# Products of 512 and of 256 columns issued in groups of six blocks that run on across the weight units, in place of groups of eight

## What is computed

```
x  = x + fox_mixer(rms_norm(x), w_in, ...) @ w_out          # 2048 -> 3*2048, 2048 -> 2048
x  = x + (silu(conv(rms_norm(x) @ w_up_gate)) * conv(... @ w_up_val)) @ w_down   # 2048 -> 2*5632, 5632 -> 2048
x  = x + concat(gla_mixer(h, ...), dilated_mixer(h, ...)) @ w_out                # the second block, same widths
x  = x + (silu(h2 @ w_gate) * (h2 @ w_up)) @ w_down
```

## Time and profile before

| | |
|---|---|
| median of 3 runs | 2276.18 us (2275.83 to 2277.05) |
| the profiled execution | 2276.7 us; its span (first to last instruction) 2274.8 us |
| TensorE matmul busy | 2260.0 us, 99% of the span, 13190 instructions |
| VectorE busy | 1623.9 us, 71% |
| ScalarE busy | 1230.4 us, 54% |
| granted TensorE clock | 0.999 of full speed over the span |
| DMA | 421.82 MB, mean 185 GB/s |

### The profile page before, as it was taken

How to read it: one execution, slowest core, us unless ns; L and a number is a source line. 1 busy time by engine, 2 the same in 40 slices (tenths; PEclk the granted TensorE clock), 3 DMA queues, 4 the chain that set the end, 5 groups by cost and what they waited for, 6 DMA issues and landing times.

```text
span 2274.8 us, 39123 instructions
## 1 busy us (share of the span) xinstructions
PE 2260.0 (99%) x13190; PEld 1980.8 (87%) x13190; DVE 1623.9 (71%) x2378; ACT 1230.4 (54%) x1614; POOL 53.1 (2%) x78
## 2 busy tenths in 40 slices
PE   8999999999999999999999999999999999999999
PEld 6888888888888888888888888888888888888888
DVE  7877777888888888555567577777666676664554
ACT  6777765655555555444465577655444444443332
POOL 1111100000000000000000000000000000000000
PEclk9999999999999999999999999999999999999999
DMA  6555555555555555655545555555555555555654
GB/s 203 193 176 183 183 169 191 187 193 191 189 192 185 193 189 186 198 194 187 192 154 187 161 168 166 168 192 190 190 193 188 190 192 188 191 191 199 203 198 134
DMA packets 118593, 421.82 MB, mean 185 GB/s; under 512 B 13773, under 2 KB 15973, under 8 KB 118544
## 3 DMA queue, kind: packets, MB, share of 16 engines
q1 hardware_dynamic: 113760, 413.19, 55.2%
q0 software_dynamic: 2048, 5.39, 0.9%
q10 hardware_dynamic: 2736, 2.58, 0.3%
HBM read 418.98 MB, written 3.70 MB: 186 GB/s over the span
## 4 chain that ended last, share of the span: by engine, by line
PE 98%; DVE 1%; ACT 0%; DMA 0%; issue 0%; SPq 0%; DVEq 0%
PE acc L378 63%; PE acc L381 32%; PE b_score L435 0%; PE b_turn L440 0%; DMA xres<-xt 0%; PE b_mean L425 0%; PE b_mean L446 0%; PE b_mean L426 0%; PE b_val L432 0%; PE b_mean L447 0%; PE b_score L434 0%; PE b_mean L448 0%; ACT xs L857 0%; PE b_mean L518 0%; PE b_mean L515 0%; PE b_score L502 0%
## 5 line engine op out<-in xcount | busy, mean ns | idle before, releaser
L729 ACT ACTIVATE whi<-raw 128x1024 fp32r<-128x1024 f32 x783 | 826.3, 1059 | 826.0 <-PE acc L381 815.1
L1053 DVE TENSOR_TENSOR wlo<-raw,whi 128x1024 fp32r<-128x1024 f32 x783 | 959.9, 1229 | 376.3 <-ACT whi L729 374.3
L378 PE MATMUL acc<-xs,whi 128*128 128x512 f32 x4344 | 1094.9, 395 | 2.2 <-DVE wlo L1053 1.8
L378 PEld LDWEIGHTS acc<-xs,whi 128*128 128x128 f32 x4344 | 781.9, 188 | 146.5 <-issue 5.1
L381 PEld LDWEIGHTS acc<-xs,wlo 128*128 128x128 f32 x4344 | 583.4, 188 | 44.3
L381 PE MATMUL acc<-xs,wlo 128*128 128x256 f32 x4344 | 593.9, 279 | 0.0
L378 PE MATMUL acc<-hid,whi 128*128 128x512 f32 x1408 | 351.0, 392 | 0.0
L1059 DVE TENSOR_REDUCE folded_t<-acc 128x256 f32<-128x512 f32 x336 | 231.9, 690 | 137.9 <-PE acc L381 128.2
L378 PEld LDWEIGHTS acc<-hid,whi 128*128 128x128 f32 x1408 | 251.9, 188 | 43.2
L381 PEld LDWEIGHTS acc<-hid,wlo 128*128 128x128 f32 x1408 | 188.3, 188 | 14.4
L381 PE MATMUL acc<-hid,wlo 128*128 128x256 f32 x1408 | 191.6, 278 | 0.0
(11 more groups left out here) (190 smaller groups left out, 1001.6 us busy)
## 6 DMA issues: line engine op xcount, KB each, us to landing
raw<-wstream SPq DMA_DIRECT2D x783, 512.0 KB, 4.0
decay_row<-decay_scratch POOLq DMA_DIRECT2D x16, 128.0 KB, 3.7
out<-xres ACTq DMA_DIRECT2D x16, 128.0 KB, 2.4
xres<-xt SPq DMA_DIRECT2D x3, 512.0 KB, 8.4
dist_scratch<-bias_scratch POOLq DMA_DIRECT2D x8, 192.0 KB, 4.6
toeplitz<-dist_scratch POOLq DMA_DIRECT2D x8, 128.0 KB, 3.9
xres<-xt SPq DMA_DIRECT2D x2, 256.0 KB, 4.6
raw<-wstream SPq DMA_DIRECT2D x2, 256.0 KB, 5.6
```

The source lines that it names most:

```text
L378: pe.matmul(acc[bank_no][:, :], w_hi, x[:, kc, :, :].rearrange("p a s -> p (a s)"), start=first, stop=False)
L729: act.activation(whi[slot][:, :], raw[slot][:, :], ACT.Copy).then_inc(hi_ready, 1)
L1053: dve.tensor_tensor(wlo[slot][:, :], raw[slot][:, :], whi[slot][:, :], ALU.subtract).then_inc(lo_ready, 1)
```

## The change

TensorE's order alone is changed: which large products stand together before their small ones. The number of products, their operands, the banks and the work of every other engine are as before. `stretch` takes the list of all blocks between two pieces of other work, whatever units they lie in, and cuts it into groups of six blocks (`GROUP`): six large products, then the six small ones of the same blocks. The first group has four blocks where the call says so (behind `head_mean`, `head_turn` and some of the linear attention's pieces). What is left at the end of a list is one group if it is three blocks or fewer, and otherwise a group of three and one of the rest: for the lists of 64 blocks (the loop bodies of `project` and `up`) and of 352 blocks (`down`) that is a group of three and a group of one. `half` alone is cut 3, 3, 2. The waits (`lo_ready` at a unit's first block, `chunk_out` at a chunk's first) now stand before the block that needs them, so in the middle of a group too, and `unit_used` rises at the small product of the unit's last block.

```diff
+GROUP = 6
-            def unit(pos, k, blocks, x):
-                slot = pos.slot(k)
-                pe.wait_ge(lo_ready, pos.unit(k) + 1)
-                for j, (bank_no, kc, first, last, late) in enumerate(blocks):
...
-                    pe.matmul(acc[bank_no][:, :], w_hi, x[:, kc, :, :].rearrange("p a s -> p (a s)"), start=first, stop=False)
-                for j, (bank_no, kc, first, last, late) in enumerate(blocks):
...
-                mm.then_inc(unit_used, 1)
+            def unit_blocks(k, bank_no, part, free=None, late=None):
 
                 late = late or {}
+                return [(k, j, bank_no, 8 * part + j, part == 0 and j == 0, part == 1 and j == 7,
+                         free if part == 0 and j == 0 else None, late.get(8 * part + j)) for j in range(BLOCKS)]
+
+            def groups(n, first=GROUP):
+                sizes = [first] + [GROUP] * ((n - first) // GROUP)
+                rest = n - sum(sizes)
+                return sizes + ([3, rest - 3] if rest > 3 else [rest])
+
+            def stretch(pos, blocks, x, first=GROUP):
+
+                at = 0
+                for size in groups(len(blocks), first):
+                    for k, j, bank_no, kc, opens, closes, free, late in blocks[at:at + size]:
+                        if j == 0:
+                            pe.wait_ge(lo_ready, pos.unit(k) + 1)
+                        if free is not None:
+                            pe.wait_ge(chunk_out, free)
+                        if late:
+                            pe.wait_ge(*late)
+                        w_hi = whi[pos.slot(k)][:, j * P:(j + 1) * P]
+                        pe.matmul(acc[bank_no][:, :], w_hi, x[:, kc, :, :].rearrange("p a s -> p (a s)"), start=opens, stop=False)
+                    for k, j, bank_no, kc, opens, closes, free, late in blocks[at:at + size]:
+                        w_lo = wlo[pos.slot(k)][:, j * P:(j + 1) * P]
+                        mm = pe.matmul(acc[bank_no][:, S:2 * S], w_lo, x[:, kc, 0, :], start=False, stop=closes)
+                        if j == BLOCKS - 1:
+                            mm.then_inc(unit_used, 1)
+                    at += size
+
+            def half(pos, k, bank_no, part, x, late=None, first=3):
+                stretch(pos, unit_blocks(k, bank_no, part, None, late), x, first)
...
-                whole_q(0)
-                whole_q(1)
+                stretch(pos, unit_blocks(k0, 1, 0, chunk - 2) + unit_blocks(k0 + 1, 1, 1), xs, 4)
                 if lag >= 2:
                     head_values(n - 2, n)
                 if lag >= 1:
                     head_scores(n - 1)
-                whole(pos, k0 + 2, 2, chunk + 1)
-                pe.wait_ge(chunk_out, chunk)
-                half(pos, k0 + 4, 3, 0, xs)
+                stretch(pos, unit_blocks(k0 + 2, 2, 0, chunk - 1) + unit_blocks(k0 + 3, 2, 1) + unit_blocks(k0 + 4, 3, 0, chunk), xs)
                 if lag >= 1:
                     head_turn(n - 1)
-                half(pos, k0 + 5, 3, 1, xs)
+                half(pos, k0 + 5, 3, 1, xs, None, 4)
...
                 with pe.Fori(1, FC // 2) as i:
-                    pairs(Pos(layer.unit_up, 8, i), i, False)
+                    stretch(Pos(layer.unit_up, 8, i), units(i, 0, 8), xs)
```

More of the change, by code:

```diff
@@ L384, in half @@
-            def half(pos, k, bank_no, part, x, late=None):
-                late = late or {}
[L387 to L393, removed]
+            def unit_blocks(k, bank_no, part, free=None, late=None):
+                late = late or {}
+                return [(k, j, bank_no, 8 * part + j, part == 0 and j == 0, part == 1 and j == 7,
+                         free if part == 0 and j == 0 else None, late.get(8 * part + j)) for j in range(BLOCKS)]
@@ L453, in head @@
                 chunk = run.chunk0 + 3 * h
-                whole_q = lambda part: half(pos, k0 + part, 1, part, xs)
-                pe.wait_ge(chunk_out, chunk - 2)
-                whole_q(0)
-                whole_q(1)
+                stretch(pos, unit_blocks(k0, 1, 0, chunk - 2) + unit_blocks(k0 + 1, 1, 1), xs, 4)
                 if lag >= 2:
@@ L530, in gla_head, with units @@
                 chunk = L1.chunk_heads + 6 * g
[L531 to L537, removed]
+                def units(lo, hi, first=GROUP):
+                    blocks = []
+                    for k in range(lo, hi):
+                        c, part = divmod(k, 2)
+                        blocks += unit_blocks(k, 1 + c % 3, part, chunk + c - 2)
+                    stretch(pos, blocks, xs, first)
@@ L539, in project @@
+                units(0, 1)
+                gla_outputs(g - 1)
+                units(1, 3, 4)
+                gla_turn_out(g - 1)
+                units(3, 8)
+                gla_intra(g)
+                units(8, 10)
+                gla_turn_v(g, True)
+                units(10, 11)
+                gla_chunk_states(g)
+                units(11, 12, 4)
             def project(layer, run):
                 last = run.count0 + run.n - 1
-                between = {0: (lambda: head_values(last - 1, last + 1), lambda: head_scores(last)),
-                           2: (lambda: head_turn(last),), 3: (lambda: pe.wait_ge(head_copied, last), lambda: head_values(last, last + 1))}
@@ L545, in group @@
[L545 to L560, removed]
@@ L562, in project, with units @@
-                group(Pos(layer.unit_out), 0, True)
+                def units(i, lo, hi, late=None):
+                    blocks = []
+                    for k in range(lo, hi):
+                        part, c = divmod(k, 4)
+                        blocks += unit_blocks(k, c, part, layer.chunk_out + 4 * i + c - 3, late if k == lo else None)
+                    return blocks
+                pos = Pos(layer.unit_out)
+                if layer.n:
+                    pe.wait_ge(g_mixed, GLA_HEADS)
@@ new lines, in project @@
+                stretch(pos, units(0, 0, 1, {0: (mix_ready, last - 1)}), mix, 4)
+                head_values(last - 1, last + 1)
+                head_scores(last)
+                stretch(pos, units(0, 1, 3), mix)
+                head_turn(last)
+                stretch(pos, units(0, 3, 4), mix, 4)
+                pe.wait_ge(head_copied, last)
+                head_values(last, last + 1)
+                stretch(pos, units(0, 4, 8, {KC - 2: (mix_ready, last), KC - 1: (mix_ready, last + 1)}), mix)
@@ L563, in project @@
                 with pe.Fori(1, KC // 4) as i:
-                    group(Pos(layer.unit_out, 8, i), i, False)
+                    stretch(Pos(layer.unit_out, 8, i), units(i, 0, 8), mix)
             def up(layer):
                 norm = 2 * layer.n + 1
[L570 to L583, removed]
@@ L585, in up, with units @@
-                pairs(Pos(layer.unit_up), 0, True)
+                def units(i, lo, hi, late=None):
+                    blocks = []
+                    for k in range(lo, hi):
+                        j, part, c = k // 4, k // 2 % 2, k % 2
+                        blocks += unit_blocks(k, 2 * j + c, part, layer.chunk_up + 4 * i + 2 * j + c - 3, late if k == lo else None)
+                    return blocks
+                pos = Pos(layer.unit_up)
+                stretch(pos, units(0, 0, 2, {0: (xs_ready, KC * norm + 8)}), xs)
@@ L586, in up @@
+                norm_mean(norm)
+                stretch(pos, units(0, 2, 8, {8 + m: (xs_ready, KC * norm + 8 + m + 1) for m in (0, 7)}), xs)
                 with pe.Fori(1, FC // 2) as i:
-                    pairs(Pos(layer.unit_up, 8, i), i, False)
+                    stretch(Pos(layer.unit_up, 8, i), units(i, 0, 8), xs)
             def down(layer):
@@ L594, in down @@
                     pe.wait_ge(hid_split, FC * (layer.n + 1) - 1)
[L595 to L604, removed]
+                    blocks = []
+                    for b in range(BLOCKS * U_DOWN // 2):
+                        c, kc = divmod(b, FC)
+                        free = layer.chunk_down + 8 * i + c - 3 if kc == 0 else None
+                        late = (hid_split, FC * (layer.n + 1)) if b == FC - 1 else None
+                        blocks.append((b // BLOCKS, b % BLOCKS, c % 4, kc, kc == 0, kc == FC - 1, free, late))
+                    stretch(pos, blocks, hid2)
             def distance_biases():
```

5 lines of the change are left out of this document (removed).

## The result

| | before | after |
|---|---|---|
| median | 2276.18 us (2275.67 to 2277.84, 13 runs) | 2281.78 us (2280.16 to 2282.74, 13 runs) |
| profiled execution, span | 2276.7, 2274.8 us | 2280.2, 2278.2 us |

The ratio is 1.0022, with a 95% interval of 1.0014 to 1.0031: the change made the kernel slower, by 5.6 us between the medians and by 3 to 7 us by the interval. The forecast was 2273, inside 2260 to 2281, and mainly "faster or no change"; it was wrong. One of the six executions of e8 took 2479.5 us at a granted clock of 0.85 in place of 1.00, and e8's ratio is without it.

A forecast was written before the change was run, and what follows sets the result against it. The prediction took TensorE's stream of products as the bound. Terms of +0.4 (loops), -2.6 (attention heads), -0.7 (linear attention and rest) and nothing for waits summed to -2.9 us, giving 2273 us, range 2260 to 2281.

The forecast's parts named there:

- What bounds the kernel: TensorE's stream of products is the bound, busy 2260.0 of 2274.8 us; only the products' pace can change the time.
- The rule on phases: In loops, large products cycle 389, 392, 395 ns (phases 1, 2, 3); a small series after phase 3 is quick.
- The loops' term, +0.4 us,: Output, up and down loops: bodies alternate 1 and 63 slow of 64; out-of-step starts add 0.4 us.
- The heads' term, -2.6 us,: 20 attention heads: 7 to 17 slow small products remain of 40 in each, saving 2.6 us over all.
- The linear heads, -0.7 us,: Four linear-attention heads and the rest: slow small products fall from some 290 to about 140, saving 0.7 us.
- Waits at nothing: Later unit releases and earlier wants are covered by the ring of buffers, and waits inside a series cost nothing.
- All quick: Rival, chance 0.30: the single small product leaves phase 1, loop bodies keep 1 slow of 64; 2262 us.
- Locked slow: Rival, chance 0.15: behind the single or a wait inside a series, phase never returns to 1; 2284 us.
- The order has no say: Rival, chance 0.10: the two paces belong to something else, such as the ring's buffers; unchanged at 2276.2 us.
- The range: Forecast range for the whole kernel, 2260 to 2281 us, leaving out most of the locked case.

The follow-up runs named there:

- e8: e5 with groups of twelve in place of six in the up and down loops, output loop keeping sixes: 2262.64 us, ratio 0.9939.
- e7: e1 with groups of twelve in place of six in the output, up and down loops: 2284.97 us, ratio 1.0041 to the kernel before.
- e1: The change with four leftover blocks cut two and two, not three and one: 2266.88 us, ratio 0.9956 to the kernel before.
- e6: e1 with one group of six ahead of each layer's up loop cut 3, 2, 1, loops untouched: 2283.71 us, ratio 1.0034.
- e10: e5 with groups of eight in the up and down loops, output loop keeping sixes: 2272.48 us, ratio 0.9982.
- e5: e1 with the 24 blocks behind the scores in each attention head cut 4, 6, 6, 6, 2: 2262.31 us, ratio 0.9938.
- e2: The change with its new groups only in the output, up and down loops, eights everywhere else: 2285.74 us, ratio 1.0041.

## Why the prediction was wrong

*What bounds the kernel* was right: the waits did not change, and the differences between all these kernels, e7's wait of half a microsecond apart, are in the pace of products. Two prices account for the spans. The loops have 70 plain bodies of 64 blocks and not 72, since the first body of each `up` holds `norm_mean`; that changes the sum little.

*The rule on phases* was right where I read it, in the loops with nothing between; e1, e6 and e10 confirm it.

*The loops' term, +0.4 us,* is the first step that failed. In `up` and `down` the bodies do alternate as I counted. What failed there is "a series that starts out of step costs about 0.01 us, once in two bodies". The price was about right, 12 ns, but how often it falls due was wrong: at each group of a slow body. A slow small series of six behind phase 2 leaves the large products at a point of the cycle at which the series of eight in these loops had not left them (one restart in each `up` before, none in `down`). Now there are 130 restarts in each `up` and 61 in each `down`, 380 more in all. At 11.2 ns they are 4.3 us, less 0.4 us for 88 slow small products fewer; the table has 4.0. That the bodies alternate was itself partly luck: the single slow product did not leave plain phase 3 but this same restart (397, 397, 392, 394, 388, 392 ns), and that series of six happens to end in phase 2 as well.

In the output loops the bodies do not alternate. I asked only what the tail of a body leaves, and not in which phase the loop is entered; the group of two ahead of it sets phase 2. 219 of 256 small products are slow there, 144 before, and 75 x 4.6 ns = 0.35 us is the 0.3 of the table.

*The heads' term, -2.6 us,* is the second. I read the entry behind `head_scores` from a kernel in which a slow series stood ahead of `head_values`. The groups of six made that series quick, and the entry moved: the six large products there end in phase 2. All 20 heads of the change have the quick series ahead and this entry. The 16 blocks behind the mean were won. Of the 24 behind the scores 16 were slow before and all are now, and each group but the first begins with a restart; the 8 behind the transposes stayed slow. So 32 products in place of 40 are slow in a head, restarts take back what that gives, and the sum is +0.1 us over 14 heads. e5 shows that four large products fit this entry. I did allow for such a shift behind the transposes, and it came; I should have allowed for it at every entry.

*The linear heads, -0.7 us,* did not come either: from the second layer's first large product to the one behind the first `head_mean` of its dilated heads it is 177.10 us before and 177.10 after. *Waits at nothing* was right in the change; e7 shows what a short wait can cost through the phase.

*The rivals.* "All quick" was reached by e1 and e5 with another tail. "Locked slow" I gave 0.15. It has the right sign, and the output loops of this kernel are locked, but they are 6 of 70 bodies and 0.6 us; most of the loss is restarts in bodies that alternate. In e2 and e6 `up` and `down` are locked. "The order has no say" is refuted by e6 alone. Products of 256 columns follow at 113 and at 118 ns in one program, so no rule by columns alone holds in these runs. The Trainium skill, page "TensorE: Matmul & The Clock Gate", section "Back-to-back issue gap", gives the formula that I used as the gap of an isolated product; for a stream of weight loads and products the same section has about 131 ns at 512 columns. I left that limit out. The traces agree with neither: here the products of 512 columns follow each other at 229 ns.

*The range* ended at 2281 because it left out most of the slower case, and the time lies 0.8 us beyond it.

## What to carry to other kernels

Where an engine is bound by issuing one kind of instruction after another, look at the starts of single instructions: a few nanoseconds that come in a cycle can be worth more than any wait. If such a cycle is found, each length in the order is a choice modulo the cycle, and so is each place where other work interrupts it; read the entry state again in the new order, since it depends on what ran before. A state that the loop itself keeps turns a small disturbance ahead of it into a cost of the whole loop, so read the state at each loop's entry as well as the one its tail leaves. A body that returns from every state would be safer; none was built here, and e1's, which keeps its state too, is slow in e6. Test one change of a group's size before a rewrite.

## What the runs showed of the hardware

- Products of 512 columns in this format follow each other at 226, 229 and 232 ns in a fixed cycle of three (rows of 389, 392, 395 ns duration), 229 on average, at full granted clock. Behind other work or a restart a series can leave this cycle: behind `norm_mean` in e1 five followed at 231 to 234 ns (396 to 398 ns duration).
- Products of 256 columns have two paces, 113 and 118 ns. Which one is fixed by the first of a series: quick if the large series ended in phase 3 of the plain cycle, else slow up to the end of the series, however long (twelve in e7). A product of 394 ns right behind one of 397 or 398 is not phase 3 in this sense; the small ones behind it are slow.
- A quick series always leaves phase 1 behind it, at lengths of 2, 3, 4, 6, 8 and 12. A slow series moves the cycle: two behind a series that began in phase 1 leave phase 2; three, six or twelve behind a series that ended in phase 1 leave phase 2; six behind a series that ended in phase 2 leave a restart of 233 and 236 ns.
- A switch between the two kinds of product has no price that these runs can tell from nothing: with groups of 3, 6 and 12 in `up` and `down` the kernel ran in 2263.23, 2262.31 and 2262.64 us, and 650 more switches for 0.9 us are at most 1.4 ns each.
- What the cycle of three is in the hardware is open; no run here tells.
